# Modulation products of two FFN stages: from TensorE matmuls to sums per partition on VectorE

## The reference, cut to what matters

```
mod = silu(c) @ ada_w[l] + ada_b[l]            # first block: (1024) x (1024, 6144), one condition
ml  = silu(c_2)   @ w_mod_2[l] + b_mod_2[l]    # second block: two conditions, latents ...
mc  = silu(c_ctx) @ w_mod_2[l] + b_mod_2[l]    # ... and context
h = rms_norm(x) * (1 + scale) + shift ;  x = x + gate * ffn(h)
ffn(h) = (silu(h @ w_gate) * (h @ w_up)) @ w_down    # 2816 hidden features; layer 1 has 8 experts instead
```

## Time and profile before

| | us |
|---|---|
| median of 3 runs | 3033.21 (3028.47 to 3035.98) |
| the profiled execution | 3029.22 |
| its span, first to last instruction | 3027.4 |
| TensorE busy | 2889.6 (95%) |
| VectorE busy | 608.1 (20%) |
| ScalarE busy | 464.1 (15%) |
| DMA, mean over the span | 208 GB/s |

### The profile page before, as it was taken

How to read it: one execution, slowest core, us unless ns; L and a number is a source line. 1 busy time by engine, 2 the same in 40 slices (tenths; PEclk the granted TensorE clock), 3 DMA queues, 4 the chain that set the end, 5 groups by cost and what they waited for, 6 DMA issues and landing times.

```text
span 3027.4 us, 39471 instructions
## 1 busy us (share of the span) xinstructions
PE 2889.6 (95%) x17906; PEld 1386.6 (46%) x17906; DVE 608.1 (20%) x1540; ACT 464.1 (15%) x997; POOL 3.8 (0%) x22
## 2 busy tenths in 40 slices
PE   6899989899999999999999997899999999978999
PEld 4457636433333333333334446444444444455784
DVE  2510016300010010100112228410000033354000
ACT  1110010200000010000013433210000023422000
POOL 0000000000000000000000000000000000000000
PEclk9999999799999999999999997899999999988999
DMA  8867685499999999999971120034342231121442
GB/s 301 318 222 251 247 315 215 169 348 345 392 344 353 389 343 391 348 349 387 341 269 56 56 70 17 1 111 165 113 167 104 104 108 56 56 84 57 139 150 72
DMA packets 290506, 630.03 MB, mean 208 GB/s; under 512 B 12153, under 2 KB 93421, under 8 KB 277918
## 3 DMA queue, kind: packets, MB, share of 16 engines
q1 hardware_dynamic: 290222, 627.29, 56.0%
q0 software_dynamic: 112, 0.17, 0.0%
HBM read 626.37 MB, written 1.05 MB: 207 GB/s over the span
## 4 chain that ended last, share of the span: by engine, by line
PE 91%; DVE 4%; DMA 1%; ACT 1%; issue 1%; SPq 1%; POOL 0%; POOLq 0%; DVEq 0%; ACTq 0%
PE banks L1397 19%; PE banks L1266 17%; PE banks L1029 10%; PE banks L1425 10%; PE banks L1306 10%; PE banks L764 3%; PE banks L960 3%; PE banks L1242 3%; PE banks L782 2%; PE banks L834 2%; PE banks L922 2%; PE banks L1085 1%; PE banks L845 1%; PE banks L1352 1%; PE banks L1374 1%; DVE sb_gate_bc L2245 1%
## 5 line engine op out<-in xcount | busy, mean ns | idle before, releaser
L1266 PE MATMUL banks<-sb_hT,sb_weights 128*128 128x256 f32 (+1 forms) x1792 | 529.9, 456 | 0.0
L1266 PEld LDWEIGHTS banks<-sb_hT,sb_weights 128*128 128x128 f32 x1792 | 338.6, 190 | 191.6 <-issue 162.7
L1397 PE MATMUL banks<-sb_weights,sb_arena 128*32 128x512 f32 x3072 | 369.6, 594 | 1.6 <-ACT sb_arena L1827 1.6
L1029 PE MATMUL banks<-sb_weights,sb_hT 128*128 128x512 f32 x736 | 323.6, 596 | 7.3 <-ACT sb_arena L1660 7.3
L1306 PE MATMUL banks<-sb_weights,sb_arena 128*128 128x512 f32 x704 | 305.7, 594 | 1.1 <-DMA sb_weights<-ffn_w_down 1.1
L1397 PE MATMUL banks<-sb_arena 128*32 128x512 f32 (+1 forms) x2560 | 285.8, 551 | 0.0
L1029 PEld LDWEIGHTS banks<-sb_weights,sb_hT 128*128 128x128 f32 x736 | 139.1, 191 | 172.9 <-issue 164.4
L1306 PEld LDWEIGHTS banks<-sb_weights,sb_arena 128*128 128x128 f32 x704 | 132.6, 190 | 169.1 <-issue 167.1
L1397 PEld LDWEIGHTS banks<-sb_weights,sb_arena 128*32 128x32 f32 x3072 | 102.3, 110 | 213.4 <-issue 211.7
L1425 PE MATMUL banks<-sb_weights,sb_hT 128*32 128x512 f32 x1536 | 168.1, 593 | 0.0
L1397 PEld LDWEIGHTS banks<-sb_arena 128*32 128x32 f32 x2560 | 85.7, 110 | 150.4 <-issue 140.7
(11 more groups left out here) (257 smaller groups left out, 2120.0 us busy)
## 6 DMA issues: line engine op xcount, KB each, us to landing
sb_weights<-moe_w_gate SPq DMA_DIRECT2D x64, 1024.0 KB, 9.6
sb_weights<-moe_w_up SPq DMA_DIRECT2D x64, 1024.0 KB, 11.9
sb_weights<-moe_w_down SPq DMA_DIRECT2D x64, 1024.0 KB, 9.1
sb_weights<-ada_w SPq DMA_DIRECT2D x48, 1024.0 KB, 9.3
sb_weights<-w_mod SPq DMA_DIRECT2D x48, 1024.0 KB, 8.7
sb_arena<-moe_w_gate SPq DMA_DIRECT2D x48, 1024.0 KB, 7.0
sb_arena<-moe_w_up SPq DMA_DIRECT2D x48, 1024.0 KB, 9.2
sb_arena<-moe_w_down SPq DMA_DIRECT2D x48, 1024.0 KB, 10.1
```

The lines of the kernel that those rows point to most:

```text
L1029: mm = pe.matmul(dst, hT[:, k, t * P:(t + 1) * P], ring[j][:, k, :], start=(k == 0), stop=(k == KC - 1))
L1266: mm = pe.matmul(dst, ring[j][:, k, lo:lo + P], hT[:, k, 0:T * P], start=(k == 0), stop=(k == KC - 1))
L1397: mm = pe.matmul(psum[32 * q:32 * q + 32, r % 2, 0:2 * w], ex_hT[:, k, g * GROUP:(g + 1) * GROUP], slot_gu[n % 7][:, k % 4, :, lo:lo + w], ...
```

## The change

`on_vector(M, n)` picks the riders that leave TensorE: all 12 loads of M = 1, all 12 of M = 3 and loads 0 to 3 of M = 2, 28 of the 32. Loads 4 to 7 of M = 2 stay. The tables change too: in stage 0 the last load of M = 1 moves from behind D0 to behind G10, and the pairs of M = 2 are one load of either kind.

For a load on VectorE, `mods_half` (called twice, for the two row blocks kk) multiplies the weights by the condition as a scalar per partition and adds them to an accumulator in SBUF (2048 floats per partition and condition), in instructions of 1024 floats: one for each half h and each condition. M = 1 has one condition, M = 2 and 3 have two. The first row block of a group is a `tensor_scalar` (TS), all others are a `scalar_tensor_tensor` (STT). The last of them gives the slot back. In step b VectorE works on the rider behind G(b-1): kk = 0 behind the product of chunk 2b, kk = 1 behind that of chunk 2b+1. The riders behind G10 and in the down steps are done one after the other once the last product is made.

For each finished group, `mods_sum` on TensorE sums the accumulator over the partitions with a stationary that has one column of ones (of 32): 4 matmuls of 512 columns in the four strips, for each condition. It stands at the end of step b (`sum_up(b)`), before the rider and the next step, for a group whose last load is behind G(b-1), and waits until VectorE has given that slot back. GpSimd sets up the stationaries with six memsets at the start.

Cut to its core:

```diff
@@ -80,8 +80,20 @@
 MOD_GROUPS = 3
 MIXER_MODS = {0: (0, (1, 2)), 1: (2, (2,))}
-GU_MODS = {0: [[], [(1, 0), (1, 1)]] + [[(1, n)] for n in range(2, 11)], 2: [[(3, n)] for n in range(11)]}
-DOWN_MODS = {0: [[(1, 11)]] + [[(2, n), (2, n + 1)] for n in (0, 2, 4, 6)], 2: [[(3, 11)]]}
+GU_MODS = {0: [[], [(1, 0), (1, 1)]] + [[(1, n)] for n in range(2, 10)] + [[(1, 10), (1, 11)]],
+           2: [[(3, n)] for n in range(11)]}
+DOWN_MODS = {0: [[(2, 4 + n), (2, n)] for n in range(4)], 2: [[(3, 11)]]}
+def on_vector(M, n):
+    return M in (1, 3) or (M == 2 and n < 4)
+def conds_of(M):
+    return (0,) if M < 2 else (1, 2)
...
@@ -440,6 +459,12 @@
             gu, down = GU_MODS.get(L, []), DOWN_MODS.get(L, [])
             return gu + [[]] * (11 - len(gu)), down + [[]] * (6 - len(down))
+        def mods_of_step(L, i):
+            return sum(mods_of_ffn(L), [])[i]
+        mod_at, summed_at = {}, {}
         def mods_of_mixer(L):
             return MIXER_MODS.get(L, (None, ()))
@@ -595,6 +620,7 @@
             def mods(loads):
                 for M, n in loads:
                     j, (g, r) = next_slot(), divmod(n, 4)
+                    mod_at[M, n] = j, (turn[int(L >= 2)] - 1) // SLOTS + 1
                     claim(j)
                     for kk in range(2):
                         sp.dma_start(slot_k2048[j][:, kk, :], ada[M][:, 2 * r + kk, g * 2048:(g + 1) * 2048])\
...
+            def skip(L):
+                g = int(L >= 2)
+                j = turns[g] % SLOTS
+                turns[g] += 1
+                c.up(landed_of(L)[j], 32)
+            def mods_sum(L, M, g, bank):
+                j, use = mod_at[M, 4 * g + 3]
+                pe.wait_ge(freed_of(L)[j], use + 1)
+                conds = conds_of(M)
+                for i, cn in enumerate(conds):
+                    for q in range(4):
+                        mm = pe.matmul(psum[32 * q:32 * q + 32, bank, :], sum_sel[:, cn, :],
+                                       mod_sums(L, i)[:, q * 512:(q + 1) * 512], start=(i == 0), stop=(i == len(conds) - 1))
+                mm.then_inc(rows_ready, 1)
+                summed_at[M, g] = c.up(rows_ready)
             def mods_load(L, r, bank):
                 j = take(L)
...
@@ -1224,8 +1270,20 @@
                 def ride(loads):
                     for M, n in loads:
+                        if on_vector(M, n):
+                            skip(L)
+                            continue
                         mods_load(L, n % 4, 6)
                         if n % 4 == 3:
+                            waiting.append((M, n // 4))
+                def sum_up(i):
+                    for M, n in mods_of_step(L, i - 1):
+                        if on_vector(M, n) and n % 4 == 3:
+                            if L == 0 and i >= 11:
+                                pe.wait_ge(hb_done, last_hidden)
+                            mods_sum(L, M, n // 4, 0 if L == 0 and i >= 11 else 6)
                             waiting.append((M, n // 4))
                 def turn_waiting():
@@ -1279,6 +1337,7 @@
                                                    hb_tok[:, at, h * P:(h + 1) * P])
                             tr.then_inc(cover_turned, 1)
                     owed.append(freed_of(L)[j])
+                    sum_up(b)
                     ride(with_gu[b])
                     s = b - len(js)
                     if s < max(T // 2, 1):
@@ -1318,6 +1377,7 @@
                         if t == 0:
                             turn_waiting()
                     owed.append(freed_of(L)[j])
+                    sum_up(11 + s)
                     ride(with_down[s])
                 if L == 0:
                     turn_tile(0, 2)
...
+                def copy_groups(i):
+                    for M, n in mods_of_step(L, i - 1) if i else ():
+                        if on_vector(M, n) and n % 4 == 3:
+                            copy_rows(0 if L == 0 and i >= 11 else 6)
+                    for M, n in mods_of_step(L, i):
+                        if not on_vector(M, n) and n % 4 == 3:
+                            copy_rows(6)
                 for n in range(4):
                     if n == cover_turn(T):
                         norm_copy(L, 1, T - 1, 4)
...
@@ -1922,6 +1987,37 @@
                              psum[:, bank, lo:lo + 48].rearrange("p (q b s) -> p q b s", q=4, b=4),
                              at(bias.to_broadcast((P, 16, 3))), ALU.add)
                 link(ins)
+            last_load = [None]
+            def mods_half(L, M, n, kk):
+                g, r = divmod(n, 4)
+                j, use = mod_at[M, n]
+                if kk == 0:
+                    dve.wait_ge(landed_of(L)[j], 32 * use)
+                    if last_load[0] is not None:
+                        given_back, at, last_group = last_load[0]
+                        dve.wait_ge(given_back, at)
+                        if r == 0:
+                            dve.wait_ge(rows_ready, summed_at[last_group])
+                    last_load[0] = freed_of(L)[j], use + 1, (M, g)
+                conds = conds_of(M)
+                for i, cn in enumerate(conds):
+                    for h in range(2):
+                        at = slice(1024 * h, 1024 * (h + 1))
+                        acc, w, by = mod_sums(L, i)[:, at], slot_k2048[j][:, kk, at], cond[:, 2 * r + kk, cn:cn + 1]
+                        if r == kk == 0:
+                            ins = TS(acc, w, by, None, ALU.mult)
+                        else:
+                            if kk:
+                                dve.wait_ge(sums_linked, c.at(sums_linked) - (2 * len(conds) - 1))
+                            ins = STT(acc, w, by, acc, ALU.mult, ALU.add)
+                        if kk and (i, h) == (len(conds) - 1, 1):
+                            ins.then_inc(freed_of(L)[j], 1)
+                        else:
+                            ins.then_inc(sums_linked, 1)
+                            c.up(sums_linked)
             def scale_columns(L, i):
                 for s in range(1 if L < 2 else 2):
@@ -2315,6 +2411,14 @@
                 for u in range(2 * cover_loads(T), FFC):
                     dve.wait_ge(silu_done, c.up(silu_done))
                     TT(ffT[:, u, :], sg[:, u % 2, :], ff_banks(u, T)[1], ALU.mult).then_inc(hb_done, 1)
+                    halves = [(M, n, kk) for M, n in mods_of_step(L, u // 2 - 1) if on_vector(M, n) for kk in range(2)]
+                    for M, n, kk in halves[len(halves) // 2:] if u % 2 else halves[:len(halves) // 2]:
+                        mods_half(L, M, n, kk)
+                for i in range(10, 11 + len(DOWN)):
+                    for M, n in mods_of_step(L, i):
+                        if on_vector(M, n):
+                            for kk in range(2):
+                                mods_half(L, M, n, kk)
                 groups = [(M, n // 4) for loads in sum(mods_of_ffn(L), []) for M, n in loads if n % 4 == 3]
                 if groups:
                     dve.wait_ge(mods_turned, c.up(mods_turned, len(groups)))
@@ -2509,6 +2613,10 @@
             pool.memset(eps[:, :], EPS)
             for n, free in enumerate(freed + freed2):
                 pool.memset(free_marks[0:1, n:n + 1], 0.0).then_inc(free, 1)
+            sel = sum_sel[:, :, :].rearrange("p s m -> p (s m)")
+            for cn in range(3):
+                pool.memset(sel[:, 33 * cn:33 * cn + 1], 1.0)
+                pool.memset(sel[:, 33 * cn + 1:min(33 * cn + 33, 96)], 0.0)
             pool.memset(ones[:, :], 1.0).then_inc(ones_set, 1)
             pool.memset(pool_bd, 0.0).then_inc(pool_cleared, 1)
             for L in stages:
```

More of the change, by code:

```diff
@@ L212, in program @@
         strip_sel = sb("strip_sel", [P, 12])
+        sum_sel = sb("sum_sel", [P, 3, 32])
         rows = sb("mod_rows", [P, 512])
@@ L262, in program, with mod_sums @@
         ybuf = view(12288, 4, D)
+        def mod_sums(L, i):
+            return mix_flat[:, 2048 * i:2048 * (i + 1)] if L == 0 else view(12288 + 2048 * i, 2048)
         diag1 = view(7552, KC, P)
@@ L349, in program @@
         mods_turned = sem("mods_turned")
+        sums_linked = sem("sums_linked")
         mods_ready = sem("mods_ready")
@@ L787, in mods_load @@
                     mm.then_inc(rows_ready, 1)
+                    c.up(rows_ready)
                 else:
@@ L1778, in ffn @@
                 sg_tok, _ = cover_space(T)
-                with_gu, with_down = mods_of_ffn(L)
+                def copy_groups(i):
[5 more added lines that the diff above has]
+                            copy_rows(6)
                 for n in range(4):
@@ L1793, in ffn @@
                             .then_inc(cover_copied, 1)
-                    for _, n in with_gu[b]:
-                        if n % 4 == 3:
-                            copy_rows(6)
+                    copy_groups(b)
                     if 0 <= b - loads < max(T // 2, 1):
                         copy_gate(b - loads, 4)
-                for loads in with_down:
```

(5 more changed lines are left out.)

## The result

The changed kernel took 3048.38 us (median of 5 runs, 3042.28 to 3051.1) against 3033.21 before: ratio 1.0047, 95% interval [1.0032, 1.0062], slower by more than 0.3%. Measured once more (c0_changed_again) it was 3054.15 (3050.31 to 3057.18) against 3031.14, ratio 1.0074 [1.0058, 1.0091]. The profiled execution of the first series took 3042.28 us and is its lowest.

What follows compares the result with a forecast made beforehand. TensorE was taken as the bound (busy 2889.6 of 3027.4 us). Stage 0 summed to +6.3 and stage 2 to +0.3, so 3033.2 + 6.6 = 3040 us, range 3026 to 3050.

Steps and rivals of the forecast that it cites:

- A: Both FFNs: 52.0 us removed, 10.3 back as sums, 38.9 as waits, 9.4 as slower clock; 0.57 including a milder-waits case.
- rival B: Slower: clock falls in every short wait and late loads take longer; 3045.5, or 3048 with slower STT; chance 0.34.
- B's first mechanism: The granted clock falls in each of the short waits too, 3.2 us over the middle value taken.
- Both pairs of sums: Gate/up steps 4 and 8: TensorE waits for VectorE's rider, 3.5 us twice in stage 0, 6.4 twice in stage 2.
- D0 waited: Stage 0's first down step: its load needs a slot VectorE holds past step 10; 10.4 us of idle TensorE.
- Rival D: Faster: VectorE runs ahead, slots return before the step's end, leaving D0's 7 us transfer; 2999; 0.09 with unseen others.
- The clock term: Stage 0: slower clock behind waits, 2.1 us for D0 and 3.1 for three short waits, the middle of 0 and 6.3.
- The ring term: Stage 0: loads queued behind a rider's held slot come late; four transfers take 12.2 us, making G7 1.9 us late.
- B's price for this: Stage 0: DMA nearer 370 GB/s makes each late load 0.5 us later, 2.2 us more in all.
- The down steps: Stage 0 after D0: D1 0.8 us late, D3 3.4 us late instead of 1.1, held by a two-condition rider's slot.

Runs made afterwards that it cites:

- e1: The changed kernel with each gate/up group's sum and copy moved from the step's end to the middle of the next step; 3032.12 us, ratio 1.0005.
- e3: The changed kernel with VectorE taking a rider up in its own step instead of the one after; 3000.78 us, ratio 0.9921.
- e2: The changed kernel with the last group of M = 1 back on TensorE and stage 0's other gate/up sums in PSUM bank 5; 3047.51 us, ratio 1.0057.
- e6: The changed kernel with only stage 2's riders on VectorE and stage 0's tables as before; 3032.58 us, ratio 1.0002.
- e8: The kernel before plus the six GpSimd memsets, unused; 3030.45 us, ratio 0.9996.
- e4: The changed kernel with unused matmuls on TensorE ahead of the four sums within the gate/up steps; 3047.6 us, ratio 1.0054.
- e5: e3 with each group's sum moved from the end of the next step to its middle; 3003.19 us, ratio 0.9909.

## Why the prediction was right and where it failed

The range (3026 to 3050) held the median of 3048.38. The likeliest case, A, did not come: the time is on rival B's side of 0.3%, 8 us above my number. That the range held is partly luck. The two FFNs, forecast to grow by 6.6 us, grew by 18.7; in the first profile "between" was 4.7 us shorter than before, without a cause in the change that any run shows, and in the second series the median, 3054.15, lies above the range although the kernel before was 2.1 us faster there. B's first mechanism, the clock in the short waits, is about half of the 11.9 us that stage 0 had beyond my sum; the other half is waits, 33.3 us for the 27.2 of my terms.

**What held.** The places of the waits. Both pairs of sums waited (3.32 for 3.5, 6.19 for 6.4); e1 and e3 take them away, and stage 2 then gives its 17 us. D0 waited 11.14 us for 10.4: SP issued it 3.3 us behind the end of step 10 (3.6 forecast) and it took 7.9 us to land (7.0 forecast); e2 shows that VectorE's slot held it. Stage 2 came out at +0.5 for +0.3, and e6 confirms it in the total. The STT took 1.28 us and two took 2.48, so they start 1.20 us apart:

```profile
246.10 2.48 DVE L2015 SCALAR_TENSOR_TENSOR sb_mixT<-sb_weights,sb_cond,sb_mixT 128x1024 f32<-128x1024 f32 x2
```

The Trainium skill (VectorE: DVE Perf Modes, "The DRAIN you can't avoid") says that the next operation does not start until the pipe is empty; an estimate by that is 2 x 1.28 = 2.56 us. The same section adds that "A next op that is not held starts earlier", which I had passed over, and the trace agrees with that. The overlap is also why VectorE was busy for 807 us in all and not near 820.

The memsets cost nothing (e8). Rival D was excluded rightly for this kernel. That e3, in which VectorE does run a step earlier, came near its number (3000.8 for 2999) is chance: D has D0's 7 us and no other wait, e3 has 0.21 us there and 12.0 us of others in stage 0.

**What failed, stage 0: predicted +6.3, measured +18.2.**

- The clock term, 5.2 predicted, 10.3 measured. I took the middle of 0 and 6.3 for three short waits (3.1) and 2.1 for D0. Behind G2 the row is 1.54 too long (8.71 for 7.17 in e3), behind both sums and G7 1.69 each, behind D0 1.58 (15.55 for 13.97 in e3), behind D3 2.16 (16.16 for 14.00): all of them, and also a wait of 2.35 us. The row I had set as the lower end, a clock still at 1.00 after 2.97 us idle, did not carry over to the short waits of this kernel. e4 shows the cause by filling the wait. The Trainium skill (TensorE: Matmul & The Clock Gate, Part 1) says that an idle TensorE falls back to 1.2 GHz. The trace agrees: over the 5 us behind each of these waits the granted clock is 0.56 to 0.69. I had let that weigh only half in the short ones.
- The ring term. "Four transfers take 12.2 us from the first issue to the last landing" was wrong by its reading: 10.0 is the median of two transfers. This is the DMA view of before for the first of them alone, which lands 9.2 us after its issue, so the last takes 10.8:

```profile
sb_weights<-ada_w SPq DMA_DIRECT2D x1, 1024.0 KB, 9.2
```

  From 263.52 to 265.9 + 10.8 is 13.2 us. After, SP issues the rider at once with G7's load, as the timeline of SP and the DMA view behind it show (KB, us to landing):

```profile
269.58 0.82 SPq L626 DMA_DIRECT2D sb_weights<-ada_w  x2
270.44 0.43 SPq L635 DMA_DIRECT2D sb_weights<-ffn_w_gate  x1
270.92 2.45 SPq L636 DMA_DIRECT2D sb_weights<-ffn_w_up  x1
```

```profile
sb_weights<-ffn_w_up SPq DMA_DIRECT2D x1, 1024.0 KB, 13.1
```

  269.58 to 270.92 + 13.1 is 14.4 us, and G7 is 3.92 us late, not 1.9. B's price for this (0.5 us a load) was too low. G2, too, took 8.3 us from issue to landing instead of 7.0: 2.35 for 1.0. G3 was milder than thought (1.80 for 2.4), and G4 was not late.
- A wait I did not see: 1.39 us (and 1.60 in stage 2) of TensorE for ScalarE's copy in the cover. Before, a rider stood in that place and filled the time, as the timeline of before shows:

```profile
212.24 1.92 PE L782 MATMUL banks<-sb_weights,sb_cond 128*32 128x512 f32 x16
214.09 1.98 PE L807 MATMUL banks<-sb_arena,sb_ones 128*128 128x512 f32 x4
```

  I costed its removal at its full length and did not ask what it covered.
- The down steps: D1 1.54 for 0.8, D3 4.52 for 3.4.

My own sum with the measured terms is −29.7 + 4.7 + 32.2 (waits of 33.3, less the old 1.1) + 10.3 = +17.5 for +18.2 measured. In stage 2 it is −22.3 + 5.6 + 14.0 + 4.6 = +1.9 for +0.5; the 1.4 us between them stay unexplained. The two stretches together grew by 18.7 us. The medians grew by 15.2 in one series and 23.0 in the other; in the two profiled executions the FFNs agree and the head differs by 7.2 us, and no run here settles what draws that.

## What to carry to other kernels

When work moves from a bound engine to an idle one, place it by when its slot is needed again, not by whether the idle engine has room: one step of delay here turned a gain of 28.7 us in the two FFNs (e3) into a loss of 18.7. In an in-order DMA queue a slot given back late also delays the loads behind it whose own slots are free, and a removed instruction may have been the cover of another engine's work. Cost a wait of TensorE of 2.3 us and more in dense work with the clock added: here it fell behind 42 of 43 such waits in the FFNs, mostly for some 1.7 us and for up to 2.9.

## What the runs showed of the hardware that was not expected

- In the FFN stretches of the thirteen profiles the granted clock over the 5 us behind an idle time of TensorE was 1.00 for every one from 1.0 to 2.07 us. Around 2.2 us it went either way: it fell behind e5's D1 (2.17) and not behind e3's D1 and G2 (2.18, 2.24). From 2.32 us on it fell behind 42 of 43, at 0.50 to 0.71. Seven of these are G2, idle 2.32 to 2.53 us, whose 32 records then took 8.71 to 8.86 us instead of 7.17. The one exception is the second sum of e2, idle 3.32 us.
- In eleven of the thirteen profiles the mean granted clock over 110 to 120 us was 0.50 to 0.70 without any idle time of TensorE, in small matmuls of the mixer; the other two are before and after of the first series. This goes with heads 2 to 8 us longer, a part of the spread between executions, and no kernel here touched that place.
- Filling a wait with unused matmuls kept the clock at 1.00 (e4): 3.3 us for two waits of stage 0, 4.6 for two of stage 2.
